# The convolution branch moved from before the merge to the first projections, and modulation rows computed in quadrants, in a two-block fp32 kernel

## The chip, the cores and the metric

The kernel runs on one core of a Trainium2 chip, as one program. The metric is the time of the whole program on the device, in microseconds; smaller is better. All data is fp32. Weight products are made from two rounded parts of each operand ("hi" and "lo", three matmuls for one product). The engines are TensorE (PE), VectorE (DVE), ScalarE (ACT), GpSimd (POOL) and SyncE (SP, which only issues the weight loads).

## What is computed

The input x has 512 tokens of 1024 columns, with a context of 256 tokens. The first block has three branches behind one normalisation and one wide projection. They are merged, and an MLP follows. A second block of two layers (MLPs, gated delta rule, attentions) comes after, and the change doesn't touch it.

```python
mod_x = jnp.split((jax.nn.silu(c) @ w_ada[l] + b_ada[l])[:, None, :], N_MOD, axis=-1)   # 6 parts of 1024
mod_c = jnp.split(jax.nn.silu(c_ctx) @ w_ada[l] + b_ada[l], N_MOD, axis=-1)
h = _rmsnorm(x, g_norm1[l]) * (1.0 + mod_x[1]) + mod_x[0]
hc = _rmsnorm(ctx, g_norm1[l]) * (1.0 + mod_c[1]) + mod_c[0]
u_rw, u_cv, u_ml, u_gate = jnp.split(h @ w_in[l], [OFF_CV, OFF_ML, OFF_GATE], axis=-1)
ya, ya_c = _rwkv_mixer(u_rw, uc_rw, ...)
yc, yc_c = _mlstm_mixer(u_ml, uc_ml, ...)
yb = _conv_branch(u_cv, cv_dw[l], cv_db[l], cv_lnw[l], cv_lnb[l], rows)
x = x + mod_x[2] * _merge(u_gate, ya, yb, yc, p_a[l], p_b[l], p_c[l], w_out[l])
h = _rmsnorm(x, g_norm2[l]) * (1.0 + mod_x[4]) + mod_x[3]

def _conv_branch(u, dw, db, ln_w, ln_b, rows):     # 512 channels, rows of 64 tokens, 31 taps
    a, g = jnp.split(u, 2, axis=-1)
    z = a * jax.nn.sigmoid(g)
    z = _depthwise_conv(z.reshape(B * rows, GRID_W, CONV_W), dw, db).reshape(B, T, CONV_W)
    return jax.nn.silu(_layernorm(z, ln_w, ln_b, LN_EPS))

def _merge(u_gate, ya, yb, yc, pa, pb, pc, wo):
    ga, gb, gc = jnp.split(jax.nn.sigmoid(u_gate), N_BRANCH, axis=-1)
    m = ga * (ya @ pa) + gb * (yb @ pb) + gc * (yc @ pc)
    return m @ wo
```

## The kernel before

Each engine has one program, written out by hand, and runs it in order; semaphores join them. The stages of the first block are: modulation parts 0 and 1 and the first norm; the matrix-LSTM projections (`pe_ml_in` and its twins); the matrix LSTM; RWKV's projections and recurrence; RWKV's output, with modulation parts 3 and 4 (`pe_rw_out`); the convolution's input projection (`pe_cv_in`); the merge (`pe_merge`); then the output projection and the MLP. `E.meet(name)` makes all engines wait for each other.

Weights come in slabs of up to 1 MB, through a ring of three slots. SP loads slab j into its slot when the slot is free. For a split slab ACT writes the rounded hi part once the slab has landed and PE has used the slot's last one, DVE writes the lo part from it, and PE waits for that. In the programs of ACT and DVE the call `E.ahead()` stands where the slab after the current one is split. So whatever DVE does ahead of such a call delays a slab's lo part. A slab of w_ada (modulation) is not split; it frees its slot when PE has used it.

`pe_fm` makes feature-major products: for each block of 128 output columns 24 matmuls (8 steps of the contraction, three for each) over 512 tokens. `pe_tm` makes token-major products, 12 matmuls per slab and token tile. ml_in has q, k (over the context too), v, o and the narrow gates g. PSUM has eight banks. `TensorLine.take` hands out the one taken longest ago and makes PE wait until its reader has freed it; `pe_tm` takes one bank for each token tile before its first matmul. ACT evicts q, k and o; DVE evicts v.

`pe_mod` makes one modulation part: two rows (latent and context) times 1024 columns, with 16 plain fp32 matmuls of two weight columns and 512 moving columns. ACT copies the rows out and eight small matmuls turn them. The norm follows: ACT squares each tile, DVE scales it, PE transposes, ACT applies scale and shift and writes hi, DVE writes lo.

The convolution has four channel blocks of 128 partitions x 512 tokens, each with 31 taps: one `tensor_scalar`, then 30 `scalar_tensor_tensor` on DVE (`dve_conv`, a generator: whoever calls `next` runs the next taps). Before, `dve_merge` runs eight taps behind each tile's product in the first four of the six parts of the merge. The norm over channels (`pe_conv_norm`: two column sums with a matrix of ones; `act_conv_norm`, `dve_conv_norm`) stands in one piece ahead of the third branch.

At RWKV's end POOL's queue loads, in this order, the constants that RWKV's buffers had overwritten, the matrix LSTM's output, the hidden state hx (both spilled to HBM earlier), rw_g2 and two norm rows. PE waits for the constants and for rw_g2.

Of the kernel before, what the change touches and what calls it, by code (L numbers as in the profile page):

```python
# [25 lines left out]
def const_tables():  # L26
# [34 lines left out]
    for d in range(2):  # L61
# [14 lines left out]
        ("gcw0", 48), ("gcw1", 48), ("qn0", 2), ("qn1", 2), ("kn0", 1), ("kn1", 1)]  # L76
# [663 lines left out]
def memory(K):  # L740
# [33 lines left out]

    A.top = mk
# [84 lines left out]
    m.yop = A.operand(4, 512)  # L860
    A.top = mk4
# [4 lines left out]
    m.yflat = K.mem[1][:, mk4 - RING:mk4 - RING + 4096]  # L866
# [105 lines left out]
def pe_mod(E, K, part):  # L972

    t, m = TensorLine(E, "mod"), K.m
    t.wait_ge(*K.at("sil"))
    for hf in range(2):
        o = t.take("mod rows", part, hf)
        for k0 in (0, 4):
            i, w, _ = t.chunk(K.I["w_ada"], 128 * k0, 4, part * 1024 + 512 * hf, 512, False)
            for k in range(4):  # L980
                keys = [("w used", i)] + ([("mod rows", part, hf)] if k0 else []) if k == 3 else []
                t.mm(o[0:2, :], m.silcv[:, k0 + k, :], w[:, k, :], k + k0 == 0, k + k0 == 7, *keys)
    o = t.take("mod", part)
    t.wait_ge(*K.at("mod rows sb", part))
    for f in range(8):
        t.mm(o[:, 2 * f:2 * f + 2], m.tmp[0:2, 128 * f:128 * f + 128], K.C["ident"][0:2, 0:2], True, True,
             *([("mod", part)] if f == 7 else []))


def act_mod(E, K, part, last=None):  # L990
    a, m = ScalarLine(E, "mod"), K.m
    if last is not None:
        a.wait_ge(*K.at("mod", last))
    for hf in range(2):
        E.ahead()
        E.ahead()
        a.wait_ge(*K.at("mod rows", part, hf))
        a.copy(m.tmp[0:2, 512 * hf:512 * hf + 512], K.bank("mod rows", part, hf)[0:2, :], ("mod rows sb", part))
        K.free(a, "mod rows", part, hf)


def dve_mod(E, K, part):
    v, m = VectorLine(E, "mod"), K.m
    for _ in range(4):
        E.ahead()
# [3 lines left out]
    K.free(v, "mod", part)  # L1009

# [6 lines left out]

def pool_first(E, K):
    g, m = PoolLine(E, "first"), K.m
    g.load(m.cst, K.I["consts"], "consts")  # L1020
    g.load(m.vec, K.I["vecs"], "vecs")
    for i in range(4):
        g.load(m.xs[:, 1024 * i:1024 * i + 1024], K.I["x"][0, 128 * i:128 * i + 128, :], "x", i)
    for i in range(2):
        g.load(m.xs[:, 1024 * (4 + i):1024 * (5 + i)], K.I["ctx"][0, 128 * i:128 * i + 128, :], "x", 4 + i)


NORM1 = (("n1", 0, 4, 0), ("n1c", 4, 2, 1))


def pe_norm1(E, K):
    t, m = TensorLine(E, "norm1"), K.m
    for st, first, n, _ in NORM1:
        pe_to_op(t, K, st, [m.xs[:, 1024 * (first + i):1024 * (first + i) + 1024] for i in range(n)], 8,
                 lambda i: (st, i, "x"))


def act_norm1(E, K):
    a, m = ScalarLine(E, "norm1"), K.m
    for st, first, n, col in NORM1:  # L1040
        for i in range(n):
            a.wait_ge(*K.at("in", "x", first + i))
            act_rms(a, K, (st, i), m.xs[:, 1024 * (first + i):1024 * (first + i) + 1024], m.scr, m.small[:, i:i + 1])
        a.wait_ge(*K.at("scale", 1))
        act_to_op(a, K, st, 8, 128 * n, (m.hL, m.hC)[col], lambda f: m.sc1[:, f, col:col + 1],
                  lambda f: m.mod[:, f, col:col + 1], m.tmp2)
        if col == 0:
            a.wait_ge(*K.at("n1", "lo", 7))


def dve_norm1(E, K):
    v, m = VectorLine(E, "norm1"), K.m
    for st, first, n, col in NORM1:
        for i in range(n):
            r, x = m.small[:, i:i + 1], m.xs[:, 1024 * (first + i):1024 * (first + i) + 1024]
            dve_rms(v, K, (st, i), r)
            v.ts(x, x, r, None, MUL, None, (st, i, "x"))
        dve_to_op(v, K, st, 8, 128 * n, (m.hL, m.hC)[col], m.tmp2)
# [8 lines left out]
def pe_ml_in(E, K):  # L1067
    t, m, W = TensorLine(E, "ml"), K.m, K.I["w_in"]
    LC = [(m.hC, 0), (m.hC, 128)] + [(m.hL, a) for a in W512]
    for k in range(8):  # L1070
        t.wait_ge(*K.at("n1", "lo", k))
        t.wait_ge(*K.at("n1c", "lo", k))
    pe_fm(t, K, "ml q", W, MLO, 512, 8, m.hL, lambda f: SEGS[0:1])
# [6 lines left out]
def act_ml_in(E, K):  # L1080
# [12 lines left out]
    a.wait_ge(*K.at("in", "spilled"))  # L1093
    for c, i, _ in tm_walk(E, 512, 8, 4):
# [11 lines left out]
def pool_ml_in(E, K):  # L1106
    g, m = PoolLine(E, "ml"), K.m
    g.load(m.gb, row(K.I["mlgb"], 16), "mlgb")
    g.load(m.nwr, row(K.I["ml_nw"][0, :], 512), "ml_nw")
    g.wait_ge(*K.at("rw hx"))  # L1110
    g.load(K.I["spill"][:, 0:8, :], m.hx1, "spilled")


def dve_ml_in(E, K):
    v, m = VectorLine(E, "ml"), K.m
    for f, _ in fm_walk(E, 512):
        if f == 0:
            v.tt(m.hx1, m.hL[:, 0], m.hL[:, 1], ADD, ("rw hx",))
    for _ in fm_walk(E, 512, lambda f: 2):
        pass  # L1120
# [2675 lines left out]
```

## Time and profile before

| | us |
|---|---|
| median of 3 runs | 4666.01 (4660.14 to 4674.2) |
| the profiled execution, device time | 4664.54 |
| its span in the trace | 4662.7 |
| PE busy | 4166.8 |
| DVE busy | 2180.1 |
| ACT busy | 1340.6 |
| mean granted TensorE clock, share of full speed | 0.928 |

The profile is of one execution. Times in the trace are counted from the start of its span. A matmul of plain fp32 leaves two records in it, a rounded one (r) one record. "Idle before" is the time an engine stood still just ahead of an instruction, and the arrow names what released it. L241 is the line through which all matmuls are issued, L295 tensor_tensor, L306 scalar_tensor_tensor, L345 ACT's activation; so the tile names and shapes tell the instructions apart: `r<-ring 128x2048` is the hi part of a slab, `r<-ring,r 128x2048` its lo part.

### The profile page before, as it was taken

The page shows a single profiled execution, that of the slowest core. Times are in us where ns is not written, and L with a number is a line of the kernel's source. Part 1 is how long each engine was busy: PE and PEld are TensorE (multiplying, and loading weights), DVE is VectorE, ACT ScalarE, POOL GpSimd, SP SyncE. Part 2 cuts the span into 40 slices and gives each one's busy share as a digit, 9 for nine tenths or more (in the row PEclk, how much of TensorE's full clock was granted, in tenths as well). Part 3 has the DMA queues.
Part 4 walks back from the last instruction along what each step waited for, and adds up shares of the span by engine and source line. Part 5 has one row for each costly group of instructions (what it writes and reads, how often), then busy time and mean ns, then how long its engine had stood idle before and what let it go on. Part 6 is the DMA issues. An engine that isn't in the chain of part 4 may idle for free.

```text
span 4662.7 us, 70153 instructions
## 1 busy us (share of the span) xinstructions
PE 4166.8 (89%) x30372; PEld 3297.4 (71%) x30372; DVE 2180.1 (47%) x2934; ACT 1340.6 (29%) x1888; POOL 157.7 (3%) x194
## 2 busy tenths in 40 slices
PE   6977968879768899999997899999999987999998
PEld 3865768865546688788766657887788766668887
DVE  2136567753764344533546445335333646444335
ACT  3134233312221322322231243223222221342222
POOL 0000011210000000000001000000000001000000
PEclk8878978989889899999999799999999988999999
DMA  5101000024113322333210103332333210113331
GB/s 196 46 1 37 18 2 3 3 77 135 63 45 122 109 96 94 91 94 96 82 55 3 64 1 104 95 96 91 91 91 100 74 37 10 56 37 95 91 100 63
DMA packets 319061, 322.12 MB, mean 69 GB/s; under 512 B 10033, under 2 KB 243553, under 8 KB 317985
## 3 DMA queue, kind: packets, MB, share of 16 engines
q1 hardware_dynamic: 312144, 287.53, 20.0%
q0 software_dynamic: 6608, 30.11, 1.7%
q8 instruction: 239, 3.92, 0.3%
q14 instruction: 70, 0.57, 0.0%
HBM read 312.37 MB, written 5.24 MB: 68 GB/s over the span
## 4 chain that ended last, share of the span: by engine, by line
PE 69%; issue 12%; DVE 12%; ACT 4%; DMA 1%; POOL 0%; DVEq 0%; ACTq 0%; SPq 0%; POOLq 0%
PE psum L241 68%; DVE ring L295 2%; DVE arena L306 2%; DVE ring L326 2%; DVE arena L295 2%; PE psum L248 1%; ACT arena L345 1%; ACT r L345 1%; ACT ring L345 1%; DVE r L295 1%; DVE arena L302 1%; DMA ring<-in_w_ada 0%; DVE arena L300 0%; DMA ring<-in_rw_g 0%; DVE arena L326 0%
## 5 line engine op out<-in xcount | busy, mean ns | idle before, releaser
L241 PE MATMUL psum<-r 128*128 128x512 f32 (+3 forms) x13056 | 2977.3, 389 | 122.4 <-DVE r L295 106.7
L241 PEld LDWEIGHTS psum<-r 128*128 128x128 f32 x13056 | 2392.2, 191 | 701.8 <-DVE r L295 79.1
L295 DVE TENSOR_TENSOR r<-ring,r 128x2048 fp32r<-128x2048 f32 (+2 forms) x269 | 580.4, 2158 | 452.4 <-ACT r L345 442.5
L345 ACT ACTIVATE arena<-psum 128x512 f32<-128x512 f32 (+3 forms) x458 | 250.3, 546 | 1249.7 <-PE psum L241 1158.0
L345 ACT ACTIVATE r<-ring 128x2048 fp32r<-128x2048 f32 (+2 forms) x269 | 484.5, 1801 | 406.1 <-PE psum L241 330.2
L241 PE MATMUL psum<-arena 64*64 64x64 f32 (+15 forms) x2400 | 399.6, 334 | 62.9 <-DVE arena L295 26.6
L241 PE MATMUL psum<-ring 64*64 64x64 f32 (+4 forms) x8608 | 351.0, 235 | 84.7 <-ACT ring L345 34.3
L241 PEld LDWEIGHTS psum<-arena 128*128 128x128 f32 (+7 forms) x2400 | 264.8, 186 | 187.8 <-issue 125.3
L241 PEld LDWEIGHTS psum<-ring 64*64 64x64 f32 (+3 forms) x8608 | 289.2, 144 | 124.5 <-issue 46.2
L295 DVE TENSOR_TENSOR arena<-arena,psum 128x512 f32<-128x512 f32 (+2 forms) x192 | 114.8, 598 | 552.6 <-PE psum L241 545.6
L241 PE MATMUL psum<-ring,arena 64*64 64x64 f32 (+6 forms) x2464 | 258.4, 289 | 100.2 <-DVE ring L295 33.0
L306 DVE SCALAR_TENSOR_TENSOR arena<-arena 128x512 f32<-128x512 f32 (+4 forms) x316 | 266.7, 844 | 119.0 <-ACT arena L345 107.7
L345 ACT ACTIVATE ring<-psum 128x512 f32<-128x512 f32 (+5 forms) x276 | 148.7, 539 | 451.2 <-PE psum L241 374.2
L241 PEld LDWEIGHTS psum<-ring,arena 64*64 64x64 f32 (+4 forms) x2464 | 147.1, 156 | 181.9 <-issue 132.2
L345 ACT ACTIVATE r<-arena 128x512 fp32r<-128x512 f32 (+1 forms) x176 | 109.4, 622 | 518.8 <-DVE arena L295 516.8
L295 DVE TENSOR_TENSOR arena<-arena 128x512 f32<-128x512 f32 (+8 forms) x289 | 176.8, 613 | 127.9 <-ACT arena L345 117.0
L241 PE MATMUL psum<-arena,ring 64*64 64x64 f32 (+6 forms) x3072 | 201.7, 255 | 32.6 <-DVE ring L295 21.9
L241 PEld LDWEIGHTS psum<-arena,ring 64*64 64x64 f32 (+4 forms) x3072 | 166.4, 161 | 61.2 <-DVE ring L295 30.1
L295 DVE TENSOR_TENSOR arena<-psum,arena 128x512 f32<-128x512 f32 (+4 forms) x112 | 71.2, 636 | 292.6 <-PE psum L241 235.0
L295 DVE TENSOR_TENSOR r<-arena,r 128x512 fp32r<-128x512 f32 (+1 forms) x176 | 119.8, 681 | 157.3 <-ACT r L345 154.4
L345 ACT ACTIVATE arena<-arena 128x512 f32<-128x512 f32 (+10 forms) x181 | 78.1, 432 | 323.1 <-DVE arena L302 168.1
L326 DVE COPY_PREDICATED ring<-arena,psum 128x512 f32<-128x512 uint32 (+1 forms) x202 | 136.0, 679 | 37.5 <-PE psum L241 30.9
(95 smaller groups left out, 1403.4 us busy)
## 6 DMA issues: line engine op xcount, KB each, us to landing
ring<-in_ffa_w_in SPq DMA_DIRECT2D x88, 512.0 KB, 5.2
ring<-in_ffb_w_in SPq DMA_DIRECT2D x88, 512.0 KB, 5.1
ring<-in_w_mlp SPq DMA_DIRECT2D x32, 1024.0 KB, 5.3
ring<-in_w_in SPq DMA_DIRECT2D x31, 1024.0 KB, 5.3
ring<-in_w_ada SPq DMA_DIRECT2D x24, 1024.0 KB, 5.2
ring<-in_mix_w_in SPq DMA_DIRECT2D x24, 1024.0 KB, 5.1
ring<-in_ffa_w_out SPq DMA_DIRECT2D x20, 1024.0 KB, 5.0
ring<-in_ffb_w_out SPq DMA_DIRECT2D x20, 1024.0 KB, 5.0
```

The costliest lines, as they stand in the source:

```text
L241: ins = self.raw.matmul(o, l, r, start=start, stop=stop, skip_group_check=True)
L248: ins = self.raw.transpose(o, i, self.K.C["ident"])
L295: self.done(self.raw and self.raw.tensor_tensor(o, a, b, f), keys)
L302: self.done(self.raw and self.raw.tensor_scalar(o, a, s1, s2, f0, f1), keys)
L306: self.done(self.raw and self.raw.scalar_tensor_tensor(out=o, in0=a, scalar=s, in1=b, op0=f0, op1=f1), keys)
L326: self.done(self.raw and self.raw.copy_predicated(o, m, d), keys)
L345: self.done(self.raw and self.raw.activation(o, i, f, scale=scale, bias=bias), keys)
```

## The change

- The convolution's input projection goes to the front of the matrix-LSTM projections, in four slabs of 256 columns (values and gates of channels 0 to 255, then of 256 to 511). The gated input z is made straight from PSUM. The context's transposes and norm slices stand behind its second slab.
- The taps run between the lo parts of the projections' slabs: 10, 10, 9, 14, 22, 22, 22 and 15. Tiles of ml v are copied out behind the last of them. The convolution's result is spilled to HBM and loaded again at RWKV's end, last on the queue.
- The norm over channels is split in steps that stand in the first three parts of the merge; its column sums stand between gate and value products of the first two parts.
- Modulation parts 0, 1, 3 and 4: each product of 128 rows is made as two of 64 rows. The four of two neighbouring k go to the four (row half, column half) positions, into two banks. ACT copies one bank out, DVE adds the other. The turning matmuls (66 rows) add the halves.
- The squares and the scaling of x stand ahead of or between the modulation's evictions, and half of the transposes between its parts. The start waits for the vectors and the identity; the other constants load behind x.
- At RWKV's end part 3 stands ahead of the gates on PE. POOL loads rw_g2 and the norm rows first, then hx, then the constants, the matrix LSTM's output and the convolution. The barriers "normed" and "convolution in" are gone.

```diff
+def pe_mod_rows(E, K, part, hf, among=BANKS):
+    o, o2 = t.take("mod a", part, hf, among=among), t.take("mod b", part, hf, among=among)
     for k0 in (0, 4):
...
+            for x in (0, 1):
+                to = 64 * (1 - x if k % 2 else x)
...
+                t.mm((o2 if k % 2 else o)[to:to + 2, :], m.silcv[HALF[x], k0 + k, :], w[HALF[x], k, :],
+                     k + k0 < 2, k + k0 > 5, *keys)
...
+def pe_first(E, K):
+    t = TensorLine(E, "norm1")
+    for n, (part, hf) in enumerate(MOD1):
+        pe_mod_rows(E, K, part, hf, among=MOD_BANKS)
+        if n == 2:
+            pe_mod_turn(E, K, 0, among=MOD_BANKS)
+            pe_turn(t, K, "n1", range(4), range(4), among=FIRST_BANKS)
+    pe_mod_turn(E, K, 1, among=MOD_BANKS)
+    pe_turn(t, K, "n1", range(4), range(4, 8))
...
+def pe_cv_in(E, K):
+    t, m = TensorLine(E, "cv"), K.m
+    for x, half in CV_PARTS:
+        pe_fm(t, K, ("cv", x, half), K.I["w_in"], CVO + 512 * x + 256 * half, 256, 8, m.hL, lambda f: SEGS[0:1],
+              ready="n1")
+        if (x, half) == (1, 0):
+            pe_turn(t, K, "n1c", (4, 5), range(8))
...
-def dve_ml_in(E, K):
+def dve_ml_in(E, K, conv):
     v, m = VectorLine(E, "ml"), K.m
...
+        taps(conv, 9 + 5 * n)
+    for _ in range(2):
+        E.ahead()
+        taps(conv, 22)
+    v.wait_ge(*K.at("in", "spilled"))
+    v.set(m.v1[:, :, :, 128:129], 1.0)
+    E.ahead()
+    taps(conv, 22)
+    E.ahead()
+    for _ in conv:
         pass
-    v.wait_ge(*K.at("in", "spilled"))
-    v.set(m.v1, 1.0)
-    for c, i, _ in tm_walk(E, 512, 8, 6):
-        v.wait_ge(*K.at("ml v", c, i))
...
+    for i in range(6):
+        v.wait_ge(*K.at("ml v", 0, i))
+        v.copy(m.v1[:, i, :, 0:128], view(K.bank("ml v", 0, i), [128, 4], [1, 128]), ("ml v1", i))
...
-    g.load(m.cst[:, m.cst_kept:], K.I["consts"][:, m.cst_kept:], "consts again")
-    g.load(m.ycT, K.I["spill"][:, 8:12, :], "ycT again")
-    g.load(m.hx2, K.I["spill"][:, 0:8, :], "hx")
     g.load(m.g2f, K.I["rw_g2"][0], "g2f")
     g.load(m.lw, row(K.I["rw_lnw"][0, :], 512), "rw_lnw")
     g.load(m.lb, row(K.I["rw_lnb"][0, :], 512), "rw_lnb")
+    g.load(m.hx2, K.I["spill"][:, 0:8, :], "hx")
+    g.load(m.cst[:, m.cst_kept:], K.I["consts"][:, m.cst_kept:], "consts again")
+    g.load(m.ycT, K.I["spill"][:, 8:12, :], "ycT again")
+    g.load(m.cvT, K.I["spill"][:, 12:16, :], "cv again")
...
+    for n, (br, pw, hf) in enumerate(MERGE):
+        pe_tm(t, K, ("mg gate", br, hf), K.I["w_in"], GO + 1024 * br + 512 * hf, 512, 8, m.hL, W512)
+        if n == 0:
+            pe_column_sums(t, K, "cv mean", m.cvT, ("in", "cv again"))
+        if n == 1:
+            pe_column_sums(t, K, "cv var", m.csq, ("cv sq",))
+        pe_tm(t, K, ("mg y", br, hf), K.I[pw], 512 * hf, 512, 4, m.yop, W512, ready=("yop", br))
```

PE at the start. `2x512` are the modulation's matmuls (of 128 rows before), L248 the transposes, `r 128x512` the projections. Before:

```order
L241 MATMUL psum<-ring,arena 2x512 x16
L241 MATMUL psum<-arena 128x2 x8
L241 MATMUL psum<-ring,arena 2x512 x16
L241 MATMUL psum<-arena 128x2 x8
L248 MATMUL psum<-arena 128x128 x48
L241 MATMUL psum<-r 128x512 x120
```

After:

```order
L241 MATMUL psum<-ring,arena 2x512 x48
L241 MATMUL psum<-arena 128x2 x8
L248 MATMUL psum<-arena 128x128 x16
L241 MATMUL psum<-ring,arena 2x512 x16
L241 MATMUL psum<-arena 128x2 x8
L248 MATMUL psum<-arena 128x128 x16
L241 MATMUL psum<-r 128x512 x96
L248 MATMUL psum<-arena 128x128 x16
L241 MATMUL psum<-r 128x512 x216
```

The first 96 projection matmuls are half of the convolution input, with the context's transposes behind them.

DVE in ml_in, from the first slab's lo part (`r<-ring,r 128x2048`) to the copies of ml v (L310). Before:

```order
L295 TENSOR_TENSOR arena<-r 128x4096
L295 TENSOR_TENSOR r<-ring,r 128x2048 x3
L330 MEMSET arena 128x3096
L295 TENSOR_TENSOR r<-ring,r 128x2048 x2
L310 COPY arena<-psum 128x4x128 x6
L295 TENSOR_TENSOR r<-ring,r 128x2048
```

After (the last third of it):

```order
L295 TENSOR_TENSOR r<-ring,r 128x2048
L306 SCALAR_TENSOR_TENSOR arena<-arena 128x512 x22
L330 MEMSET arena 128x24
L295 TENSOR_TENSOR r<-ring,r 128x2048
L306 SCALAR_TENSOR_TENSOR arena<-arena 128x512 x6
L302 TENSOR_SCALAR arena<-arena 128x512
L306 SCALAR_TENSOR_TENSOR arena<-arena 128x512 x15
L295 TENSOR_TENSOR r<-ring,r 128x2048
L306 SCALAR_TENSOR_TENSOR arena<-arena 128x512 x15
L310 COPY arena<-psum 128x4x128 x6
L295 TENSOR_TENSOR r<-ring,r 128x2048
```

The taps (L306) now stand between the slabs' lo parts and ahead of the copies.

DVE in the merge, behind a value product. Before:

```order
L295 TENSOR_TENSOR arena<-arena,psum 128x512
L295 TENSOR_TENSOR arena<-arena 128x512
L306 SCALAR_TENSOR_TENSOR arena<-arena 128x512 x8
L295 TENSOR_TENSOR arena<-arena,psum 128x512
L295 TENSOR_TENSOR arena<-arena 128x512
L306 SCALAR_TENSOR_TENSOR arena<-arena 128x512 x8
```

After, in the first two parts:

```order
L295 TENSOR_TENSOR arena<-arena 128x2048 x2
L295 TENSOR_TENSOR arena<-arena,psum 128x512 x4
L295 TENSOR_TENSOR r<-ring,r 128x2048 x3
L295 TENSOR_TENSOR arena<-arena,psum 128x512 x4
L302 TENSOR_SCALAR arena<-psum 128x512
```

The taps are gone and steps of the norm over channels have come in.

## Rows read from the trace of the kernel before

**Rows 1.** The page, busy time, share of the span and instructions of each engine

```profile
PE 4166.8 (89%) x30372; PEld 3297.4 (71%) x30372; DVE 2180.1 (47%) x2934; ACT 1340.6 (29%) x1888; POOL 157.7 (3%) x194
```

**Rows 2.** Groups by shape, merge: busy us, mean ns | idle before, releasers

```profile
L241 PE MATMUL psum<-r 128*128 128x512 f32 x864 | 212.5, 408 | 59.7 <-DVE r L295 58.2 <-DVE arena L295 1.5
...
L241 PE MATMUL psum<-arena 128*128 128x512 f32 x16 | 11.0, 851 | 17.7 <-DVE arena L306 12.3 <-DVE arena L295 5.5
```

**Rows 3.** Timeline of PE in the merge: start, us, instruction, count [idle before]

```profile
1205.10 36.11 PE L241 MATMUL psum<-r 128*128 128x512 f32 x144 [15.18 <-DVE r L295]
...
1349.14 5.76 PE L241 MATMUL psum<-arena 128*128 128x512 f32 x8 [12.27 <-DVE arena L306]
1360.39 5.26 PE L241 MATMUL psum<-arena 128*128 128x512 f32 x8 [5.48 <-DVE arena L295]
...
1395.51 45.33 PE L241 MATMUL psum<-r 128*128 128x512 f32 x192 [2.17 <-DVE r L295]
```

**Rows 4.** Timeline of DVE in the merge, the end of its second part

```profile
1247.69 6.26 DVE L306 SCALAR_TENSOR_TENSOR arena<-arena 128x512 f32<-128x512 f32 x8
1253.87 4.68 DVE L295 TENSOR_TENSOR r<-ring,r 128x2048 fp32r<-128x2048 f32 x2
```

**Rows 5.** Timeline of all engines from the modulation to the first projection

```profile
34.27 13.89 PE L241 MATMUL psum<-ring,arena 128*2 128x512 f32 x32
...
41.39 0.59 ACT L345 ACTIVATE arena<-psum 2x512 f32<-2x512 f32 x1 [9.04 <-PE psum L241]
...
58.70 0.78 ACT L345 ACTIVATE arena<-psum,arena 128x512 f32<-128x512 f32 x1 [1.60 <-PE psum L248]
...
61.71 0.69 DVE L295 TENSOR_TENSOR r<-arena,r 128x512 fp32r<-128x512 f32 x1 [0.84 <-ACT r L345]
...
86.13 1.91 ACT L345 ACTIVATE r<-ring 128x2048 fp32r<-128x2048 f32 x1 [0.54 <-DVE r L295]
...
86.37 142.69 PE L241 MATMUL psum<-r 128*128 128x512 f32 x672 [6.71 <-ACT r L345]
```

**Rows 6.** Timeline of PE from RWKV's end to the convolution input

```profile
1045.10 19.72 PE L241 MATMUL psum<-ring,arena 128*128 128x512 f32 x40 [22.70 <-DMA ring<-in_rw_g]
1065.49 1.94 PE L241 MATMUL psum<-arena 2*128 2x2 f32 x16 [0.68 <-ACT arena L345]
...
1083.96 3.48 PE L248 MATMUL psum<-arena,ring 128*128 128x128 f32 x16
1093.75 46.68 PE L241 MATMUL psum<-r 128*128 128x512 f32 x192 [6.30 <-DVE r L295]
```

**Rows 7.** Two windows: busy us by engine (PE, PEld, DVE, ACT, POOL), clock, DMA share, GB/s

```profile
20.00:25.00 5.00, 4.44 (x11) 0.77 (x10) 0.00 (x0) 0.59 (x1) 0.00 (x0) 1.00 1.03 400
...
1035.00:1040.00 5.00, 0.00 (x0) 0.00 (x0) 3.35 (x7) 1.33 (x2) 0.00 (x0) 0.50 1.02 421
```

**Rows 8.** Timeline of PE in RWKV, 3 of 56 records that follow in fours

```profile
989.81 0.22 PE L241 MATMUL psum<-arena,ring 64*64 64x64 f32 x1
...
989.83 0.22 PE L241 MATMUL psum<-ring,arena 64*64 64x64 f32 x1
989.86 0.22 PE L241 MATMUL psum<-arena,ring 64*64 64x64 f32 x1
```

**Rows 9.** The 24 loads of w_ada, from issue to landing

```profile
DMA to landing us min/median/max: 5.1/5.2/23.3
```

**Rows 10.** The context's norm, timeline; then groups by shape in ml_in, 86 to 229

```profile
78.86 0.43 DVE L295 TENSOR_TENSOR r<-arena,r 128x256 fp32r<-128x256 f32 x1 [0.68 <-ACT r L345]
...
L241 PE MATMUL psum<-r 128*128 128x16 f32 x144 | 28.5, 344 | 0.0
...
L295 DVE TENSOR_TENSOR arena<-r 128x4096 f32<-128x4096 f32 x1 | 4.4, 4419 | 0.0
L310 DVE COPY arena<-psum 128x512 f32<-128x512 f32 x6 | 4.2, 692 | 23.3 <-PE psum L241 23.3
```

More of the change, by code:

```diff
@@ L992, in act_mod, with act_mod_rows @@
+MOD_ROWS = (slice(0, 2), slice(64, 66))
+def act_mod_rows(a, K, part, hf, last=None):
+    m = K.m
+    a.wait_ge(*K.at("mod zero", part))
     if last is not None:
         a.wait_ge(*K.at("mod", last))
[L994 to L1005, printed above, removed]
+    a.wait_ge(*K.at("mod rows", part, hf))
+    for x in MOD_ROWS:
+        a.copy(m.tmp[x, 512 * hf:512 * hf + 512], K.bank("mod a", part, hf)[x, :], ("mod rows a", part, hf))
+    K.free(a, "mod a", part, hf)
@@ L1006, in dve_mod, with dve_mod_rows, dve_mod_turn @@
+def dve_mod_rows(v, K, part, hf):
+    m = K.m
+    v.wait_ge(*K.at("mod rows a", part, hf))
+    for x in MOD_ROWS:
+        o = m.tmp[x, 512 * hf:512 * hf + 512]
+        v.tt(o, o, K.bank("mod b", part, hf)[x, :], ADD, ("mod rows sb", part))
+    K.free(v, "mod b", part, hf)
+def dve_mod_turn(v, K, part):
+    m = K.m
     v.wait_ge(*K.at("mod", part))
@@ L1009, in dve_mod, with act_mod @@
     K.free(v, "mod", part)
+def act_mod(E, K, part, last=None):
+    a = ScalarLine(E, "mod")
+    for hf in range(2):
+        E.ahead()
+        E.ahead()
+        act_mod_rows(a, K, part, hf, last=last)
 def dve_scale(E, K, sc, part, g):
@@ L1024, in pool_first @@
     for i in range(2):
[L1025 to L1048, printed above, removed]
@@ L1051, in dve_norm1 @@
[L1051 to L1058, printed above, removed]
+        g.load(xtile(K, 4 + i), K.I["ctx"][0, 128 * i:128 * i + 128, :], "x", 4 + i)
+    g.load(m.cst[:, 128:], K.I["consts"][:, 128:], "consts")
@@ new lines, in dve_cv_in @@
+def dve_cv_in(E, K, conv):
+    v, m = VectorLine(E, "cv"), K.m
+    for x, half in CV_PARTS:
+        E.ahead()
+        for f in range(2) if x else ():
+            b = 2 * half + f
+            v.wait_ge(*K.at("cv g sb", half, f))
+            v.tt(m.z[b][:, :, 15:79], h8(K.bank(("cv", 0, half), f, 0)), h8(m.cacc[:, b, :]), MUL, ("cv z", b))
+            K.free(v, ("cv", 0, half), f, 0)
+        if (x, half) == (1, 0):
+            n = VectorLine(E, "norm1")
+            for f in range(8):
+                dve_turned(n, K, "n1c", 256, 1, f)
+        elif half:
+            taps(conv, 10)
@@ L2027, in dve_rw_out @@
     v.ts(s[:, 0:32], s[:, 0:32], 1.0 / 64, 64e-5, MUL, ADD, ("rw n", "var"))
+    for _ in range(8):
+        E.ahead()
+    for hf in range(2):
+        dve_mod_rows(mod, K, 3, hf)
     v.wait_ge(*K.at("rw n", "sd"))
@@ L2056, in pe_rw_out @@
     t, m = TensorLine(E, "rw"), K.m
+    K.fences[E.slab] = K.late[E.slab] = "RWKV done"
+    pe_mod(E, K, 3)
     t.wait_ge(*K.at("in", "g2f"))
```

402 lines of the change are left out of this document (225 added, 177 removed).

## The prediction

> **What bounds the kernel now.** I read the page first: over the span PE is busy 89% and DVE 47% [rows 1], so an edit pays only where PE stands still. Next comes the table of instruction groups for the stretch from 1141.9 us (the merge begins) to 1441: PE has 864 projection matmuls there, 212.5 us of work, with 59.7 us of idle time before them, and 17.7 us before the 16 records of the convolution's column sums [rows 2]: 77.4 us idle in 299. The PE timeline shows the form of it: stops of 15.2, 12.3 and 5.5 us, each released by DVE, while the last 192 matmuls run through in 45.33 us, 0.236 us each [rows 3]. The DVE timeline says what DVE does then: eight taps of the convolution take 6.26 us (0.78 each) behind every tile's product, and the low parts of the next two weight slabs (4.68 us, 2.34 each) come only behind them [rows 4]. PE makes a tile's product in 12 matmuls, 2.8 us. DVE needs 7 to 8 us a tile, so it bounds every second part of the merge.
>
> **The merge after.** No tap stands in it. PE has 864 x 0.236 = 204.0 us, and the same eight column-sum matmuls (16 records), now in two groups of four: a plain fp32 matmul of 512 columns takes 0.87 (13.89 us for the 16 matmuls of one modulation part, two records each [rows 5]), so 6.9. The first group fills PE's wait for the first operand split; before the other two splits PE waits as now, 2.17 us each [rows 3], 4.3. After an idle stretch the clock starts low: the 192 matmuls at 1093.75 took 46.68 [rows 6] plus a stop where the rate gives 45.33; I charge 1.9. Sum 217.1 us. DVE's norm steps (three of 2.3, a reciprocal of 3.4) go behind products, where DVE has over 15 us free in each part of 34.
>
> **RWKV's end.** Now PE waits 22.7 us for rw_g2, to 1045.10, makes gates and both modulation parts, and starts the convolution input at 1093.75 [rows 6]. After, rw_g2 is loaded first, but PE still waits for the constants to come back, and these now stand behind rw_g2, two norm rows and hx, 2.8 MB. DMA moves about 420 GB/s here with all its engines busy [rows 7], shared with the w_ada slabs: the constants land near 1045. The wait stays, on another load. From there, an estimate by that rate: the GpSimd queue has 6.6 MB to load, 1 MB more than before, so w_ada's slab 3 is in at 1054 and part 3's rows are done at 1055.7; ACT and DVE evictions 2.4; turn 1.94 [rows 6]; four gates 3.4: 1063.6. Slab 7 can be asked for only when slab 4 is used: it lands at 1070.5, the rows are done at 1072.2, evictions take 2.4, DVE's eight low parts of h 6.3 and three small operations 0.6: 1081.5. PE's 16 transposes (3.48 [rows 6]) and ACT's copies end beside that. DVE now waits for part 3's rows ahead of its own normalisation (12 operations, 8.7 us), and the gate products wait behind both; that ends near 1070, before slab 7's rows, and costs nothing while they are late. As now, 5.1 us pass from there to the first projection matmul: 1086.6, which is 7 us sooner. With w_ada at its full rate it would be 13, with the loads 7 us later 0.
>
> The convolution input is gone from here, so the merge ends at 1086.6 + 217.1 = 1303.7. Now it ends at 1395.51 + 45.33 = 1440.8 [rows 3]. **Minus 137.1.**
>
> **The start.** PE's first projection is at 86.37 now [rows 5]. A w_ada slab takes PE 3.47 us now (13.89 for four [rows 5]), and 1.7 if four quadrants work at a time. That they can is shown in the RWKV stage: 64 x 64 matmuls start four within 0.02 us and the next four 0.05 us after the first, two cycles for each of their 64 columns [rows 8]. PE then waits for DMA, which moves 400 GB/s with all engines busy while x and the constants load [rows 7]; one w_ada slab took 23.3 us [rows 9]. By 9.8 MB at that rate slab 3 lands at 28, slab 5 two slabs of 2.6 us later, at 33.3. Part 1's first half ends at 35.0; a turn and 16 transposes bring 40.4; the last half 43.8; ACT 2 x 0.59 [rows 5], DVE as much, the turn and three small operations: at 49.0 ACT starts to normalise, against 58.70 now [rows 5]. The squares and the scaling of x, now behind the modulation, are done under it. The first slice takes 1.4, the first weight slab's high part 1.91, seven slices 1.55 each, the last low part 0.7 [rows 5]: 64.0. PE's first block follows slice by slice to 65.2, the second ends at 72.8 (5.7 and 1.9 for the clock), the next two at **T = 84.1**.
>
> From T on **DVE sets the pace**. The eight slices of the context's norm step by 0.43 + 0.68 = 1.11 us [rows 10], so the low part of slab 11 is done at T + 14.2. Behind it, in the order shown, come 120 taps x 0.78 and four first ones at 0.6 (96.2), seven low parts of 2.34 (16.4), three small operations (1.7), a wait for the last gate block (1.9) and the sum of hi and lo of the hidden state, 4.4 [rows 10]: T + 134.8. Only then do the copies of ml v come, 0.69 each [rows 10]. PE's own work up to that point is 3.5 of transposes, 22.7 of convolution input and 142.69 [rows 5] less ml o (22.7) less ml g (28.5 [rows 10]): T + 117.7. ml o takes four PSUM banks, two of which hold tiles 0 and 1 of ml v, and these are emptied only behind the last tap, at T + 136.4. **PE waits some 19 us**, a few of them already at slabs 13, 14, 17 and 18, whose low parts stand behind 7 to 17 us of taps. The low clock behind the stop costs 1.9, ml o 22.7, ml g 28.5: T + 189.5 = 273.6. Now the stage ends at 86.37 + 142.69 = 229.1 [rows 5]. **Plus 44.5.**
>
> **Sum.** On the profiled execution's device time (4664.5; its span is 4662.7): 4664.5 + 44.5 - 137.1 = **4572 us**, rounded. The median shown is 4666.0, 0.03% above it; I add nothing for that. What follows the merge has the same instructions as before and is counted at nothing.
>
> **A rule that speaks against the quadrants.** In the RWKV stage four matmuls run at a time, and the code there sends both row halves into one PSUM bank, in different partitions [rows 8]. The Trainium skill, TensorEngine Tiling (Array Packing), "Gotcha 1: PSUM Pressure", says: "Different row tiles cannot access same PSUM bank simultaneously". The new modulation does the same: the two row halves of one k write one bank, at partitions 0 and 64. By the rule only two would run at a time, which is rival 1 by pairs, 4588; by the trace all four do, 4572.
>
> **Rivals.**
> 1. The quadrants overlap less than fully: two output columns in each and 512 moving ones, where [rows 8] has 64 and 64. By pairs a slab costs 3.4 us as now: plus 7.5 at the start (six slabs behind DMA) and 8 at RWKV's end, 4588. Not at all: 6.9 a slab, plus 31 and 32, 4635. For it: no row has such a shape. Against it: [rows 8]. Chance 0.13.
> 2. DVE keeps up and PE never waits at ml o: 19 us less, 4553. That needs taps 0.16 us cheaper than 0.78. Against it: [rows 4] has the same operation on the same shape. Chance 0.07.
> 3. The taps hide nowhere: low parts stand behind taps at every slab and ACT's high parts behind PE, so that all 96 us are on the path instead of 19: 4649. Against it: at ml k and the first half of ml v a low part is done 1 to 4 us before PE needs it, by my sum; that is thin. Chance 0.03.
> 4. **Slower than before.** TensorE's clock stays at the lower level through convolution input and ml_in, since PE meets a gap at nearly each slab. A wide matmul then costs 0.21 us more, of 624, and 96 narrow ones half of that: 141; the 19 us of waiting are absorbed: 4694. It passes today's time when some 80% of these matmuls run so. Against it: in the merge, with stops of 15 us, 144 matmuls still took 36.11, 0.25 each [rows 3]. Chance 0.02.
> 5. Something else holds: the convolution's result, last on its queue, comes late for the merge (it is in by about 1053 at [rows 7]'s rate, 30 us early), or the start's loads are served in another order. 4600 to 4665, chance 0.03.
>
> **How the numbers follow.** The forecast has 0.72. Its own bounds: the wait before ml o 14 to 25, RWKV's end 0 to 13 gained, the start 5 either way, clock phases 5 either way: 4553 to 4592. The range takes in rival 2 and rival 1 by pairs: **4550 to 4604**. About 0.3%, 14 us, is what a measurement of this kernel can tell from no change: below 4652 is faster. Rival 4, and a part of 3 and 5, lie above that: faster 0.94, same 0.03, slower 0.03.
>
> **What will show it.** After: the merge's 864 matmuls have under 8 us of idle time before them and the merge lasts 215 to 220; PE stands up to 20 us before the first matmul of ml o, released by a DVE copy (if not, rival 2); a w_ada slab's 16 records take 1.7 us (if 3.4 or 6.9, rival 1); PE's wait ahead of part 3's rows, behind RWKV, is released by the constants' load; the merge begins near 1131 on the new axis. It is wrong if the projections end before 262 or after 285, or if the clock is low there for more than two blocks.

## The result and the profile after

| | before | after |
|---|---|---|
| median of 4 runs, us | 4666.0 (4660.1 to 4674.2) | 4556.6 (4552.3 to 4563.3) |
| span of the profiled execution, us | 4662.7 | 4550.3 |
| mean granted TensorE clock in it | 0.928 | 0.933 |

The ratio is 0.9766, 95% interval 0.9746 to 0.9785: **109 us faster**; the time is 15 us below the forecast and inside the range. But the sum came out near for a mixed reason: two steps of it gave less than I said, and some 27 us came from a place where I had written "counted at nothing". The profiled execution of the changed kernel is the fastest of its four.

The page of the changed kernel: the span, then busy time, share and instructions of each engine (as [rows 1]), and the chain that ended last, by engine:

```profile
span 4550.3 us, 70452 instructions
...
PE 4105.8 (90%) x30500; PEld 3291.3 (72%) x30500; DVE 2187.2 (48%) x2955; ACT 1343.4 (30%) x1893; POOL 158.2 (3%) x197
...
PE 78%; DVE 13%; ACT 4%; issue 3%; DMA 1%; POOL 0%; DVEq 0%; ACTq 0%; POOLq 0%
```

PE has 128 records more than before and is busy 61 us less. No edit of the diff takes work from PE except the quadrants, so either the clock or the pace of the same matmuls has changed. I come back to that.

**The merge.** Groups by shape from 1125.6 to 1355.5 us (busy us, mean ns | idle before), to hold against [rows 2], and PE's timeline (start, us, instruction, count [idle before]) against [rows 3]:

```profile
L241 PE MATMUL psum<-r 128*128 128x512 f32 x864 | 209.2, 404 | 15.0 <-DVE r L295 13.3 <-DVE arena L302 1.7
L241 PE MATMUL psum<-arena 128*128 128x512 f32 x16 | 7.2, 592 | 0.0
```

```profile
1130.91 24.83 PE L241 MATMUL psum<-r 128*128 128x512 f32 x96 [5.38 <-DVE r L295]
...
1209.01 22.64 PE L241 MATMUL psum<-r 128*128 128x512 f32 x96 [1.71 <-DVE arena L302]
1233.81 24.18 PE L241 MATMUL psum<-r 128*128 128x512 f32 x96 [2.17 <-DVE r L295]
1261.54 46.56 PE L241 MATMUL psum<-r 128*128 128x512 f32 x192 [3.54 <-DVE r L295]
1310.26 45.21 PE L241 MATMUL psum<-r 128*128 128x512 f32 x192 [2.16 <-DVE r L295]
```

77.4 us of idle time have become 15.0, and 5.38 of those stand ahead of the merge. It lasts from 1130.91 to 1355.5.

**The start and the projections.** PE's timeline:

```profile
8.03 3.59 PE L241 MATMUL psum<-ring,arena 64*2 64x512 f32 x16 [8.03 <-DMA arena<-in_consts]
12.22 2.12 PE L241 MATMUL psum<-ring,arena 64*2 64x512 f32 x16 [0.60 <-DMA ring<-in_w_ada]
...
29.44 7.18 PE L241 MATMUL psum<-ring,arena 64*2 64x512 f32 x48 [6.34 <-DMA ring<-in_w_ada]
...
46.84 3.53 PE L241 MATMUL psum<-arena 66*128 66x2 f32 x16 [2.85 <-DVE arena L295]
...
119.60 11.26 PE L241 MATMUL psum<-r 128*128 128x512 f32 x48 [0.51 <-DVE r L295]
133.30 50.55 PE L241 MATMUL psum<-r 128*128 128x512 f32 x264 [2.43 <-DVE r L295]
184.62 17.04 PE L241 MATMUL psum<-r 128*128 128x512 f32 x72 [0.77 <-DVE r L295]
217.13 51.73 PE L241 MATMUL psum<-r 128*128 128x512 f32 x240 [15.47 <-DVE arena L310]
```

A slab's 16 quadrant records take 3.59 us after an idle stretch and 2.12 otherwise (1.89 at RWKV's end, below). The wait ahead of ml o is there, released by DVE's copy of ml v (L310), 15.47 us; the projections end at 268.86.

**RWKV's end.** PE's timeline, against [rows 6]:

```profile
1083.92 7.59 PE L241 MATMUL psum<-ring,arena 64*2 64x512 f32 x48 [23.94 <-DMA arena<-in_consts]
1093.45 1.89 PE L241 MATMUL psum<-ring,arena 64*2 64x512 f32 x16 [1.93 <-DMA ring<-in_w_ada]
1098.10 3.54 PE L241 MATMUL psum<-arena 66*128 66x2 f32 x16 [2.75 <-DVE arena L295]
...
1113.81 1.89 PE L241 MATMUL psum<-ring,arena 64*2 64x512 f32 x16 [1.64 <-DMA ring<-in_w_ada]
1118.55 3.46 PE L241 MATMUL psum<-arena 66*128 66x2 f32 x16 [2.85 <-DVE arena L295]
```

**Behind the merge.** With the first load of w_mlp as a mark (SP's timeline: 1548.7 before, 1465.3 after) 3114.0 us were left before and 3085.0 are left after: 29 us less, for the same instructions. (w_mlp is the MLP's first weight; its load marks the same point in every trace.) To see why, I put two stretches of the second block side by side that have nothing in them but full-width products: 80 us of an MLP's input stage (`pe_fm`; hL, the hi and lo parts of the hidden state, moving) and 28 us of its output stage (`pe_tm`, the weight slab moving). Windows (busy us of PE and its records, granted clock, DMA share, GB/s), before and then after:

```profile
2173.30:2253.30 80.00, 80.00 (x345) 1.00 0.30 90
2257.30:2285.30 28.00, 28.00 (x121) 1.00 0.36 113
```

```profile
2082.40:2162.40 80.00, 80.00 (x351) 1.00 0.32 94
2166.40:2194.40 28.00, 28.00 (x121) 1.00 0.40 123
```

PE is busy throughout, the granted clock is 1.00 in both, and yet in the first stretch six more products fit into 80 us. From start to start a product of 128x512 takes 233.3 ns before and 228.9 after on average (single distances 230 to 235 and 225 to 232); in the second stretch 234.2 and 233.3. At 2.4 GHz and one column a cycle, an estimate, 512 columns are 213.3 ns. Behind the w_mlp mark some 9,370 distances between such products (those below 245 ns) have a mean of 233.59 ns before and 230.74 after, which is 26.7 us of the 29.

What differs for these instructions? Not the diff's code, but one line of it that my front part had passed over: the table of small vectors got eight columns.

```diff
-        ("gcw0", 48), ("gcw1", 48), ("qn0", 2), ("qn1", 2), ("kn0", 1), ("kn1", 1)]
+        ("gcw0", 48), ("gcw1", 48), ("qn0", 2), ("qn1", 2), ("kn0", 1), ("kn1", 1), ("two", 8)]
```

The tiles are laid one behind another, so hL and all behind it (hop and hop1, which hold the left operands of the output stages, too) moved up by 32 bytes.

### The profile page after: what moved, and what is told of

Its sections match the earlier page's. It is cut to its first block, busy times and chain, and to the rows that moved or that the text cites. A ratio compares the mean times of both kernels' runs of the same rounds, so it can differ in the third digit from the quotient of the medians.

```text
span 4550.3 us, 70452 instructions
## 1 busy us (share of the span) xinstructions
PE 4105.8 (90%) x30500; PEld 3291.3 (72%) x30500; DVE 2187.2 (48%) x2955; ACT 1343.4 (30%) x1893; POOL 158.2 (3%) x197
## 4 chain that ended last, share of the span: by engine, by line
PE 78%; DVE 13%; ACT 4%; issue 3%; DMA 1%; POOL 0%; DVEq 0%; ACTq 0%; POOLq 0%
PE psum L241 77%; DVE ring L295 3%; DVE arena L306 2%; DVE ring L326 2%; DVE arena L295 2%; PE psum L248 2%; ACT ring L345 1%; ACT arena L345 1%; ACT r L345 1%; DVE r L295 1%; DMA ring<-in_w_ada 1%; DVE arena L302 1%; DMA arena<-in_consts 1%; DVE arena L300 0%; DVE arena L326 0%
## 5 line engine op out<-in xcount | busy, mean ns | idle before, releaser
L241 PE MATMUL psum<-r 128*128 128x512 f32 (+3 forms) x13056 | 2943.0, 387 | 85.7 <-DVE r L295 60.5
L345 ACT ACTIVATE arena<-psum 128x512 f32<-128x512 f32 (+5 forms) x462 | 252.6, 547 | 1142.8 <-PE psum L241 1055.8
L295 DVE TENSOR_TENSOR arena<-arena,psum 128x512 f32<-128x512 f32 (+3 forms) x208 | 125.8, 605 | 588.8 <-PE psum L241 542.4
L241 PE MATMUL psum<-ring,arena 64*64 64x64 f32 (+6 forms) x2592 | 239.0, 317 | 110.2 <-DVE ring L295 33.0
L306 DVE SCALAR_TENSOR_TENSOR arena<-arena 128x512 f32<-128x512 f32 (+4 forms) x316 | 266.7, 844 | 117.4 <-ACT arena L345 106.4
L295 DVE TENSOR_TENSOR arena<-arena 128x512 f32<-128x512 f32 (+6 forms) x285 | 174.2, 613 | 105.6 <-ACT arena L345 95.9
```

The source lines that it names most:

```text
L241: ins = self.raw.matmul(o, l, r, start=start, stop=stop, skip_group_check=True)
L295: self.done(self.raw and self.raw.tensor_tensor(o, a, b, f), keys)
L306: self.done(self.raw and self.raw.scalar_tensor_tensor(out=o, in0=a, scalar=s, in1=b, op0=f0, op1=f1), keys)
L345: self.done(self.raw and self.raw.activation(o, i, f, scale=scale, bias=bias), keys)
```

## The experiments

The runs came in three groups, each with its own runs of the kernel before (medians of seven: 4667.8, 4670.5, 4667.8). Each variant has four runs; medians below.

### Does the pace hang on the tiles' place?

`b_pad8`, the kernel before with the tiles moved by 32 bytes and nothing else:

```diff
     m.st6 = al(16)
+    al(8)
     mk_h = A.top
```

> The kernel before with 8 unused words between st6 and hL, so that hL and all the tiles behind it in the arena move up by 32 bytes, as they do in the changed kernel (whose vecs grew by the 8 columns of "two"). Nothing else differs. The two traces differ behind the merge where the instructions are the same: the 128x512 products with hL as the moving operand follow each other every 233.3 or 234.3 ns in the trace before and every 228.9 ns in the trace after, and the span lost 27.4 us there. Theory (place of the tiles): 228.9 ns here too wherever hL moves, and 22 to 30 us less than before: 4640. Rival (the order of the slots or banks, or the moment of the run): 233.3 and 234.3 ns stay, 4666, within 3 us.

Measured: **4640.5** (4637.6 to 4647.3), ratio 0.9942 (0.9927 to 0.9958), 27 us faster than before. The same two windows:

```profile
2159.80:2239.80 80.00, 80.00 (x351) 1.00 0.31 93
2243.80:2271.80 28.00, 28.00 (x121) 1.00 0.40 122
```

The counts and the distances (228.9 and 233.3 ns) are those of the changed kernel.

`a_pad8`, the changed kernel with the same edit, which puts hL back to 32 bytes off a multiple of 64:

> The changed kernel with the same 8 words, so that hL is back on the kind of address that it has in the kernel before (a multiple of 32 bytes, not of 64). Theory (place of the tiles): 233.3 and 234.3 ns are back, 4556 + 27 = 4583. Rival (order of slots and banks, moment of the run): 228.9 ns stays, 4556.

Measured: **4585.4** (4582.9 to 4586.7), ratio 0.9820 (0.9804 to 0.9836). 344 products in the 80 us, 233.3 ns. Up to the merge this run is as fast as the changed kernel: its projections end at 268.80 and w_mlp is asked for at 1463.5, not 1465.3. In the changed kernel DVE sets the pace of the projections, so PE's better pace is worth nothing there; it pays behind the merge.

The theory stands, the rival (order of slots, moment of the run) falls. How much the places give behind the merge is read best without the two stretches of delta rule and attention, whose clock differs from trace to trace (below, under the wait ahead of ml o). Without them the time from the w_mlp mark to the end is 2021.3 us before, 1995.0 after, 1996.9 in `b_pad8` and 2016.5 in `a_pad8`. So 26.3 of the 29 us are the places' for certain; 2.7 lie in those stretches, which hold some full-width products too, and there place and clock can't be told apart. That `b_pad8`'s whole gain is 27 us too is partly chance: in its trace 7.2 us of it arise ahead of the mark and 24.4 behind, and delta rules and attentions give 8.9 back.

`a_pad16` and `a_pad112` ask for which distance:

> The changed kernel with 16 unused words: hL moves by 64 bytes. Theory, if a multiple of 64 bytes is what counts: 228.9 ns and 4556, no change. If the next multiple (128 bytes) counts for more: below 228.9 ns, down to 213.3 ns (512 columns at 2.4 GHz), up to 150 us less. Rival (place counts for nothing): 4556.

> The changed kernel with 112 unused words: hL then starts on a multiple of 512 bytes. Theory, if a multiple of 64 bytes is what counts: the same as the changed kernel, 4556. If a larger multiple counts: faster than with 16 words. Rival (place counts for nothing): 4556.

Measured: **4570.6** (4567.6 to 4576.9) and **4535.9** (4534.1 to 4538.0). So "a multiple of 64 bytes" was wrong: with 16 words the input stages fell back to 233.3 ns and the output stages improved to 228.9. With 112 the input stages ran at 226.7, the output stages stayed at 233.3. What orders both stages alike is the distance between moving and stationary operand. The slabs start on multiples of 256 bytes; so in an input stage the moving operand stands above the stationary one by hL's remainder, and in an output stage below it by hop's. `c_align0` takes both remainders to 0:

```diff
+    al(112)
     mk_h = A.top
...
+    al(48)
     mk_y = A.top
```

> The changed kernel with 112 unused words ahead of hL and 48 more ahead of the tiles behind it, so that hL (the moving operand of the fm stages) and hop1, hop, yop (the stationary operands of the tm stages) all start on a multiple of 256 bytes. With 112 words alone hL's stages ran at 226.7 ns for a product of 128x512 and hop's at 233.4. Theory (the pace follows the distance of the moving operand's address from the stationary one's, modulo 256 bytes, best at 0): about 3000 products go from 233.4 to 226.7, 4535.9 - 20 = 4516. Rival (only the moving operand's place counts): 4536.

Measured: **4518.7** (4515.2 to 4523.4), ratio 0.9677 (0.9663 to 0.9692). Windows as above:

```profile
2071.70:2151.70 80.00, 80.00 (x354) 1.00 0.33 98
2155.70:2183.70 28.00, 28.00 (x125) 1.00 0.48 150
```

Both stages are at 226.7 ns, and the time behind the mark, counted as above, is 1965.4 us. `a_pad104` has the last of the eight distances:

> The changed kernel with 104 unused words ahead of hL: the moving operand's address then stands 56 words (modulo 64) above the stationary one's in the fm stages and in the tm stages alike, the one of the eight distances that no kernel has had yet. The paces so far: 226.7 ns at 0, 228.9 at 16, 233.3 at 8, 24 and 32, 234.3 at 40, 233.4 at 48. Theory (0 is the best, its neighbours are poor): about 233.3 ns and 4585 (4580 to 4592). Rival (the pace follows no such distance): one stage keeps 226.7 to 229 and the time is below 4565.

Measured: **4588.9** (4587.9 to 4591.3), 233.3 and 233.2 ns. The whole table, in words of 4 bytes, from the starts of successive products in the traces:

| moving minus stationary, modulo 64 words | input stage | output stage |
|---|---|---|
| 0 | 226.7 (a_pad112, c_align0) | 226.7 (c_align0) |
| 8 | 233.3 (before) | |
| 16 | 228.9 (after, b_pad8) | 228.9 (a_pad16) |
| 24 | 233.3 (a_pad8) | 233.3 (a_pad8) |
| 32 | 233.3 (a_pad16) | 233.3 (after, b_pad8) |
| 40 | | 234.2 (before) |
| 48 | | 233.3 (a_pad112) |
| 56 | 233.3 (a_pad104) | 233.2 (a_pad104) |

Where a distance has an entry in both columns they agree to 0.1 ns. That is what speaks for the distance: the slabs always start on multiples of 256 bytes, so no run moved both operands together, and two separate rules, one for each operand's own remainder, would fit as well. That the two operands' reads get into each other's way is a reading that suggests itself, and isn't shown. Even at distance 0 a product takes 13 ns more than the estimate for its columns.

### What is the change worth, places apart?

`b_align0` gives the kernel before the same good places (120 and 48 words):

> The kernel before with its tiles on multiples of 256 bytes (120 and 48 unused words), so that neither kernel has the advantage of its addresses. From the changed kernel at 40 and 24 bytes' remainders in words (4585.4) to the one on 256 bytes (4518.7) it was 66.7 us, and the kernel before has a pace of 234.3 ns in its tm stages on top (some 5 us). Theory: 4667 - 71 = 4596, so that the change by itself, addresses apart, is worth 4596 - 4519 = 77 to 85 us and not 110. Rival (place and change are not independent): below 4580 or above 4610.

Measured: **4596.3** (4590.4 to 4601.1), ratio 0.9849 (0.9834 to 0.9863). Against `c_align0` the change is worth 78 us. In the other pairs with one pace in their input stages it is 84 (`b_pad8` to the changed kernel, 228.9 ns) and 82 (before to `a_pad8`, 233.3 ns). The three differ by less than the runs of one kernel do (the changed kernel's four by 11 us). One reason for a smaller gain on good places is in the traces: there the kernel before asks for w_out 13.5 us earlier than it did, and the changed one only 2.8.

### The wait ahead of ml o

`a_behind`:

```diff
     E.ahead()
-    for _ in conv:
-        pass
     for i in range(6):
         v.wait_ge(*K.at("ml v", 0, i))
         v.copy(m.v1[:, i, :, 0:128], view(K.bank("ml v", 0, i), [128, 4], [1, 128]), ("ml v1", i))
         K.free(v, "ml v", 0, i)
-    for _ in tm_walk(E, 512, 8, 4):
+    E.ahead()
+    taps(conv, 12)
+    E.ahead()
+    for _ in conv:
         pass
```

> The changed kernel with DVE's last 25 taps put behind its six copies of the matrix LSTM's v (12 between the lo parts of ml o's second slab and of ml g's slab, the rest behind both). In the changed kernel PE waits 15.47 us for those copies before ml o. Theory (DVE is late there by the taps that it still has): the wait falls to 0 to 3 us and nothing else becomes late, since DVE has little to do during ml o: 4556.6 - 14 = 4543. Rival (the taps are then late for the next step instead: sigmoids of o, gates): 4553 to 4557.

PE's timeline at ml o:

```profile
203.81 51.65 PE L241 MATMUL psum<-r 128*128 128x512 f32 x240 [3.75 <-DVE arena L310]
```

The wait is 3.75 us and the projections end at 255.46 instead of 268.86: 13.4 sooner, as expected. But the time is **4550.9** (4546.9 to 4553.8), ratio 0.9743 (0.9726 to 0.9759): 5.7 less, not 14. Following the loads on SP's timeline, this trace is 11.4 us ahead of the changed kernel's all through the merge and 11.7 at 2159 (the stretch from RWKV's last matmul to the merge took 74.3 us instead of 70.9). Then comes the first delta rule. Windows over it and over the second layer's (busy us of PE, PEld, DVE, ACT, POOL; clock; DMA share, GB/s), of the changed kernel and then of `a_behind`:

```profile
2170.90:2518.00 347.10, 293.64 (x3850) 230.97 (x3849) 205.74 (x286) 88.25 (x122) 21.08 (x19) 0.91 0.13 40
3522.00:3869.40 347.40, 293.12 (x3850) 231.69 (x3849) 205.61 (x286) 88.25 (x122) 21.09 (x19) 0.91 0.13 40
```

```profile
2159.20:2513.20 354.00, 299.51 (x3851) 234.86 (x3850) 205.87 (x286) 88.38 (x122) 20.61 (x19) 0.88 0.13 39
3520.90:3868.30 347.40, 292.99 (x3850) 231.27 (x3850) 205.58 (x286) 88.25 (x122) 21.10 (x19) 0.91 0.13 40
```

Same instructions, same DVE and ACT time; the granted clock is 0.88 instead of 0.91 and the stage takes 6.9 us more. The attentions behind it took 3.8 more. In the second layer the same stage is back at 347.4. Over the traces of the changed kernel and the four variants with the same places it lasts 347.1 to 354.9 us, with the clock between 0.91 and 0.88 (over all traces up to 356.5). The runs of one kernel go the same way: the changed kernel's four, 4552.3, 4556.0, 4557.2 and 4563.3, had mean clocks of 0.933, 0.932, 0.931 and 0.929. With one trace of each kernel it can't be told whether an edit or the single execution decides it. Nor is half the gain lost for good: the same edit on top of `c_align0` is worth 10.5 us (`d_best`, below), and the two traces compared here are the slowest of `a_behind`'s four runs and the fastest of the changed kernel's.

### How much do the taps cost where they are?

`a_notaps` leaves out 29 of the 31 taps in each block (its result is another function):

> The changed kernel without 29 of the 31 taps of each block of the convolution (the first and the last are computed, the others left out), everything else in place: what the taps still cost where they are now. Theory (they hide but for DVE's lateness: 15.5 us ahead of ml o and part of 4.0 us at the slabs): 4556.6 - 18 = 4538. Rival (what is gained there is partly given back by the clock behind it, as with the taps behind the copies): 4545 to 4552. Rival (they slow the other engines or the transfers beside them): below 4530.

Measured: **4540.0** (4533.9 to 4542.5), ratio 0.9726 (0.9712 to 0.9741). Its projections run without a stop:

```profile
96.64 149.72 PE L241 MATMUL psum<-r 128*128 128x512 f32 x720 [0.37 <-DVE r L295]
```

They end at 246.36, 22.5 us before the changed kernel's. The 116 taps left out, some 87 us on DVE at 0.752 each, cost 22.5 there: 19.5 of waits and 3 of what lies around them. At w_out the trace is still 22.2 us ahead; of the whole time 16.6 are left, since delta rules and attentions took 9.8 more.

### The quadrants, and the constants

`a_rows128` makes the modulation's rows as before, in their new place (per product, and ACT copies one bank alone):

```diff
-            for x in (0, 1):
-                to = 64 * (1 - x if k % 2 else x)
-                ...
-                t.mm((o2 if k % 2 else o)[to:to + 2, :], m.silcv[HALF[x], k0 + k, :], w[HALF[x], k, :],
-                     k + k0 < 2, k + k0 > 5, *keys)
+            t.mm(o[0:2, :], m.silcv[:, k0 + k, :], w[:, k, :], k + k0 == 0, k + k0 == 7, *keys)
```

> The changed kernel with the modulation's rows in the form of the kernel before: one product of 128 rows for each 128 rows of the slab, one bank, no additions on DVE, everything else in its new place. Theory (four quadrants run at once, as 16 records in 1.9 us for a slab show, against 8 records of 0.434 us = 3.5 us in the kernel before): 1.6 us for each of the slabs at the high clock, up to 3.4 at the low one, about half of the 16 slabs on the path: 4556.6 + 12 to 25, so 4573. Rival (slabs are paced by their landing alone): 4557, within 3. Rival (the turn and its additions cost more than the quadrants save): below 4553.

Measured: **4567.4** (4565.2 to 4568.6), ratio 0.9780 (0.9766 to 0.9795), 10.9 more than the changed kernel; that misses my 12 to 25 narrowly. By the marks only 2 us of it arise at the start and 4 in all by the merge (w_out is asked for 3.8 later). The rest comes in the delta rules and attentions (11.7 more in this trace). So the quadrants save 1.6 us a slab where PE could go on, but the slabs are paced by their landing, and some 4 us are left.

`a_consts` lets PE go ahead of the constants:

```diff
-    E.wait_ge(*K.at("in", "consts again"))
     pe_rw_out(E, K)
+    E.wait_ge(*K.at("in", "consts again"))
```

> The changed kernel with PE's wait for the constants that come back moved from ahead of the modulation rows at RWKV's end to behind them, ahead of the merge, whose column sums are the first to read them. In the changed kernel PE waits 23.94 us there with slabs landed. Theory: it starts at the first slab's landing, some 13 us sooner, frees the slots sooner, and then waits for slabs, since the DMA rings are full until 1085 in either case: 4 to 12 us less, 4549. Rival (the bytes that have to land set the end in any case): 4556, within 2.

Measured: **4558.2** (4553.8 to 4560.5), ratio 0.9760 (0.9745 to 0.9775): no change, the rival. PE's timeline shows one wait split up into waits for slabs:

```profile
1068.33 3.59 PE L241 MATMUL psum<-ring,arena 64*2 64x512 f32 x16 [8.41 <-DMA ring<-in_w_ada]
1078.18 3.59 PE L241 MATMUL psum<-ring,arena 64*2 64x512 f32 x16 [6.26 <-DMA ring<-in_w_ada]
1089.16 5.91 PE L241 MATMUL psum<-ring,arena 64*2 64x512 f32 x32 [7.38 <-DMA ring<-in_w_ada]
...
1112.00 1.90 PE L241 MATMUL psum<-ring,arena 64*2 64x512 f32 x16 [1.72 <-DMA ring<-in_w_ada]
```

The last slab's rows begin 1.8 us sooner than in the changed kernel. In both traces the DMA engines are busy (share 0.97 and more) from 1065 to 1100, whether PE waits or not, so the bytes decide.

### The two gains together

`d_best` has the places of `c_align0` and the taps of `a_behind`:

> The changed kernel with the tiles on multiples of 256 bytes (112 and 48 unused words) and with DVE's last 25 taps behind the copies of v: the two edits that were faster alone. If their gains add: 4518.7 - 5.7 = 4513; if the 13 us that the second took off the projections come through whole: 4506. Rival (the clock in the delta rules and attentions, which took half of the second edit's gain, takes all of it): 4519.

Measured: **4508.2** (4500.3 to 4509.0), ratio 0.9656 (0.9642 to 0.9671), 48 us below the changed kernel, 10.5 below `c_align0`, and the fastest of all.

## Why the prediction was right, and where it wasn't

**What bounds the kernel, the merge's idle time**: right. Of the 77.4 us 15.0 are left now that no tap stands in the merge, none of them behind a tap.

**The merge after, 217.1 us**: too low, 224.6. The term that was mis-sized is "before the other two splits PE waits as now, 2.17 us each". Two waits more came: 1.71 ahead of the third part, for the bank that DVE's new norm step (L302) frees, and 3.54 in the fourth, ahead of its second gate slab, whose lo part stood on DVE behind the reciprocal (3.35 us) and a product of 2.3. They are 5.3 of the 7.5 us. The step that failed is "go behind products, where DVE has over 15 us free": free on average, but the next slab's lo part stood behind them. The trace of before has a wait of the same kind, behind the norm in its old place:

```profile
1380.34 13.00 PE L241 MATMUL psum<-r 128*128 128x512 f32 x48 [3.49 <-DVE r L295]
```

The rest is the clock, low at the merge's beginning: the first 96 products took 24.83 us, where 0.236 each gives 22.7, and the 16 column-sum records 7.2. Two of the signs that I had named, under 8 us of idle time ahead of the 864 matmuls and a merge of 215 to 220, so didn't come true.

**RWKV's end, 7 us sooner**: wrong, 0.4. From RWKV's last matmul to the merge it took 71.35 us before (1022.40 to 1093.75 [rows 6]) and 70.9 after. The constants did release PE, at 23.94 us instead of my 22.6, and slab 3 came 2 us later than written. Behind slab 3 the clock fell to its lower level again (granted 0.50 from 1098.16 to 1104.99): the turn took 3.54 instead of 1.94 and the four gates 5.3 instead of 3.4. So slab 4 was used later, and slab 7, which waits for that, was done 5.9 us after my time. That is the step that failed: turn and gates sized at the higher clock. Behind slab 7's rows I had 14.4 us, without a second turn; it took 15.2, with a turn of 3.46 in it. I had named 0 as the bound of this term and taken the middle. In the traces of the changed kernel and of the eight variants that alter nothing there, this stretch takes 70.5 to 74.3 us, so the new order at RWKV's end gained nothing.

**The start, T = 84.1**: right within a microsecond (PE's next records, behind the convolution input's second slab, start at 83.05). ACT began to normalise at 51.08, not 49.0, because the second turn was slow, 3.53; the last blocks made up for it.

**DVE sets the pace, PE waits some 19 us**: right in mechanism and size. 15.47 ahead of ml o, 4.0 at the slabs, ending 268.86 against 273.6; a tap took 0.752 us and not 0.78, which is 3.4 us over 120 (the mean of the 120 taps in the trace of before is 0.752 too; I had taken one row of eight). Rival 2 had asked for 0.16 less. `a_behind` shows that the copies' place behind the taps was the reason.

**Sum up to the merge's end.** The front 6.9 us better by RWKV's last matmul (37.6 late, not 44.5), RWKV's end 6.6 worse, the merge 7.5 worse: 85.4 us ahead of the kernel before at that point, where I had 92.6. Of the 6.9, 4.7 are there when the projections end; the other 2.2 come in the stretch from there to RWKV's last matmul, which takes 788.7 to 793.4 us over all traces without an order that I can see. That the merge began at 1130.91, where I had written "near 1131", is luck: the first two errors cancel.

**"What follows the merge has the same instructions as before and is counted at nothing"**: this step failed, by 27 us. The same instructions are not the same time when their operands have moved. `b_pad8` (27 us faster by the places alone) and `a_pad8` (29 slower) show it from both sides. Places apart, the change is worth 78 to 84 us by the pairs above, and I had forecast 94: what stands in the forecast gave less than it said, and an accident that isn't in it made up for that. Nothing in the rows of before could have told its sign; that a full-width product took 233 ns and not 213 was there to be asked about.

**Rivals.** 1, by pairs or not at all: the rows refute both, 16 records in 1.9 to 2.1 us. Here the trace is at odds with the sentence of the Trainium skill (TensorEngine Tiling (Array Packing), "Gotcha 1: PSUM Pressure") that I had weighed: the two row halves write one bank at partitions 0 and 64, and the four still go at the pace of four. 3, taps that hide nowhere: of the 87 us of taps that `a_notaps` leaves out 22.5 were on the path. 4, low clock: the clock was 1.00 from 100 to 183; it was 0.76 from 183 to 269, over the wait, ml o and the narrow ml g. 5 didn't occur: the convolution's column sums have no idle time before them.

## What to carry to other kernels

When PE is busy but a product takes longer than its columns at the granted clock, look at where moving and stationary operand start: here their remainders modulo 256 bytes were worth 27 us by accident and 38 more on purpose, which cost 160 unused words. When the front of a kernel changes, compare the traces stage by stage and the far stages too, or a shift in memory is booked as the change's merit. And work put on an engine with time to spare belongs behind what frees banks for PE, not ahead of it.

## What the runs showed of the hardware

- **The pace of full-width products goes with the operands' addresses.** 226.7 to 234.2 ns at a granted clock of 1.00, in the table above. The Trainium skill (TensorE: Matmul & The Clock Gate, "Step-by-step: what each phase is for") says: "Loading the next tile's weights doesn't steal SBUF read bandwidth from the running matmul." No run here tests that sentence, since none takes the load away; which of the reads costs the time is open. What the runs show is that a product with its own load takes 13.4 to 20.9 ns over the 213.3 of the estimate, and that the part above 13.4 changes with 32 bytes.
- **The clock in the delta rules differs for the same instructions.** 0.88 to 0.91 for the same 3850 records, 347 to 357 us, different between the two layers of one execution (354.0 and 347.4 in `a_behind`). A gain of 5 us ahead of such a stage can't be read from one trace's end; from its marks ahead of the stage it can.
- **Row halves into one bank.** A slab's eight quadrant products, 2 columns each by 512 moving ones, take 1.89 to 2.12 us at the high level of the clock; their 16 records start in fours, 0.43 us apart. The four products of 128 rows that they replace took 3.47 (0.87 each, two records of 0.434 [rows 5]).
